# Input projections by token tiles: units of 512 weight columns and half the contraction instead of 256 columns and all of it

## The reference

```
even:  p = h @ w_in          # 1024 x 3072
       q, k, v, g, u, sv = split(p, 6)      # 512 columns each
odd:   p = h @ w_in          # 1024 x 2608
       q  = rope(p[..., :1024]);  kv = p[..., 1024:2560]  (cmp, sel, win: k 256, v 256 each; k gets rope)
       gates = sigmoid(p[..., 2560:])       # 48
```

## Time and profile before

| | us |
|---|---|
| three runs, median | 1634.25 |
| lowest, highest | 1633.77, 1636.83 |
| span of the profiled execution | 1633.6 |
| TensorE busy | 1589.3 (97%) |
| VectorE busy | 797.2 (49%) |
| ScalarE busy | 679.8 (42%) |
| GpSimd busy | 229.6 (14%) |

### The profile page before, as it was taken

How to read it: one execution, slowest core, us unless ns; L and a number is a source line. 1 busy time by engine, 2 the same in 40 slices (tenths; PEclk the granted TensorE clock), 3 DMA queues, 4 the chain that set the end, 5 groups by cost and what they waited for, 6 DMA issues and landing times.

```text
span 1633.6 us, 31861 instructions
## 1 busy us (share of the span) xinstructions
PE 1589.3 (97%) x13307; PEld 1453.7 (89%) x13307; DVE 797.2 (49%) x1314; ACT 679.8 (42%) x1302; POOL 229.6 (14%) x574
## 2 busy tenths in 40 slices
PE   8999999999999999999999899999999999999998
PEld 7999988699999999998999666667989999999997
DVE  5755452556531555337334576743165552355523
ACT  3222134455532554324332566654355552354522
POOL 3000010300000000002013345432020000000001
PEclk9999999999999999999999999999999999999999
DMA  7222328122233232332334400034202323323231
GB/s 223 83 75 78 104 73 206 25 78 77 84 93 99 78 84 80 94 95 54 112 106 92 167 16 2 1 94 99 80 27 78 87 69 103 95 82 99 58 89 55
DMA packets 187417, 138.50 MB, mean 85 GB/s; under 512 B 11376, under 2 KB 178576, under 8 KB 187248
## 3 DMA queue, kind: packets, MB, share of 16 engines
q1 hardware_dynamic: 179424, 113.26, 24.4%
q0 software_dynamic: 7888, 23.79, 5.2%
HBM read 128.21 MB, written 13.01 MB: 86 GB/s over the span
## 4 chain that ended last, share of the span: by engine, by line
PE 89%; DVE 5%; ACT 2%; POOL 1%; issue 1%; DMA 1%; POOLq 0%; SPq 0%; DVEq 0%; ACTq 0%
PE gemm L990 42%; PE gemm L648 18%; PE gemm L659 9%; PE misc L623 6%; PE gemm L1132 2%; PE misc L1163 2%; PE misc L721 1%; PE gemm L707 1%; DVE y L1727 1%; PE misc L1283 1%; PE gemm L745 1%; PE misc L745 1%; PE gemm L677 1%; DVE wL L1693 1%; DMA xin<-in_x_prompt 1%
## 5 line engine op out<-in xcount | busy, mean ns | idle before, releaser
L1693 DVE TENSOR_TENSOR wL<-raw,wH 128x2048 fp32r<-128x2048 f32 (+2 forms) x107 | 222.1, 2076 | 222.8 <-ACT wH L1318 222.7
L990 PE MATMUL gemm<-hH,wH 128*128 128x272 f32 x1280 | 268.5, 291 | 0.1
L990 PE MATMUL gemm<-hH,wL 128*128 128x272 f32 x1280 | 264.8, 288 | 0.0
L990 PE MATMUL gemm<-hL,wH 128*128 128x272 f32 x1280 | 264.0, 288 | 0.0
L990 PEld LDWEIGHTS gemm<-hH,wH 128*128 128x128 f32 x1280 | 200.5, 188 | 6.2 <-issue 4.9
L1318 ACT ACTIVATE wH<-raw 128x2048 fp32r<-128x2048 f32 (+2 forms) x107 | 185.2, 1731 | 48.3 <-PE gemm L648 31.1
L990 PEld LDWEIGHTS gemm<-hL,wH 128*128 128x128 f32 x1280 | 201.0, 188 | 0.0
L990 PEld LDWEIGHTS gemm<-hH,wL 128*128 128x128 f32 x1280 | 200.0, 189 | 0.0
L1959 DVE SCALAR_TENSOR_TENSOR conv<-up,rows_t,conv 128x560 f32<-128x560 f32 x88 | 70.6, 802 | 209.2 <-ACT conv L1318 209.2
L1318 ACT ACTIVATE up<-gemm 128x32 f32<-128x32 f32 (+2 forms) x264 | 66.0, 324 | 176.0 <-PE gemm L990 153.7
L648 PE MATMUL gemm<-hH,wH 128*128 128x272 f32 (+1 forms) x624 | 133.0, 294 | 0.8 <-issue 0.5
(11 more groups left out here) (370 smaller groups left out, 2849.1 us busy)
## 6 DMA issues: line engine op xcount, KB each, us to landing
raw<-in_f_w_in SPq DMA_DIRECT2D x88, 512.0 KB, 5.0
raw<-in_f_w_out SPq DMA_DIRECT2D x32, 704.0 KB, 4.6
raw<-in_e_w_in SPq DMA_DIRECT2D x12, 1024.0 KB, 5.2
raw<-in_o_w_in SPq DMA_DIRECT2D x10, 1024.0 KB, 5.2
raw<-in_e_w_out SPq DMA_DIRECT2D x4, 1024.0 KB, 6.4
raw<-in_o_w_out SPq DMA_DIRECT2D x16, 256.0 KB, 6.4
pages<-in_cache_cmp POOLq DMA_DIRECT2D x10, 256.0 KB, 4.8
xin<-in_x_prompt SPq DMA_DIRECT2D x2, 1024.0 KB, 7.7
```

Source lines behind the costliest of these rows:

```text
L990: ins = pe.matmul(gemm[odd][:, n, 0:TH], w, x[:, k, n * TH:(n + 1) * TH], start=(k == 0 and part == 0), stop=(k == nk - 1 and part == 2))
L1693: order(dve.tensor_tensor(unit_view(wL, u), unit_view(raw, u), unit_view(wH, u).bitcast(F32), ALU.subtract), lo_ready)
```

## The change

The token units become pairs. A pair has 512 weight columns, and its two units ("parts") hold one half of the contraction each (k-blocks 0 to 3, then 4 to 7). A part moves 512 columns per matmul, 4 k-blocks x 3 x 4 tiles. The four prompt tiles take the four gemm banks, one each (`token_bank`), and stay there from part 0 to part 1; only part 1 has chunks (4), so its tiles are copied out one by one. The number of units stays as it is: 4 in the even layer, 10 in the odd one.

The sample tokens are four f32 matmuls of 512 columns per part, in bank b4, at the start of a part; in the very first part of each layer they come after the tiles. They replace tile 0 in the first units too. SyncE's load of unit u+2 waits for the sample matmuls of unit u in all parts now. A part 0 waits for VectorE's sum of the pair before (`sample_ev`). ScalarE's wait for part 0 is a semaphore of its own (`part_done`).

On VectorE the sample rows are 512 wide and come once per pair; the ropes of a q pair (two groups of 4 heads) both follow the pair's last tile. In the even layer `sample_rows` of the `v` pair moves out of the layer norm to ahead of its scaling. In the odd layer ScalarE takes the four turned blocks in one go after the high half of unit 5, and TensorE waits for the first of them ahead of unit 4 (`cp_ev`). The transposes of `vcPt` move to bank b6.

```diff
-    for n in (10, 11, 4, 5, 0, 1, 2, 3, 8, 9, 6, 7):
-        units.append(("even_in", 0, n, 5 if n in (4, 5, 10, 11) else 2))
+    def by_tokens(kind, columns):
+        return [(kind, 0, (columns, part), 4 * part) for part in range(2)]
+
+    units = by_tokens("even_tok", 2560) + by_tokens("even_tok", 1024)
+    for n in (0, 1, 2, 3, 8, 9, 6, 7):
+        units.append(("even_in", 0, n, 2))
...
+    for columns in (1024, 1536, 2048):
+        units += by_tokens("odd_tok", columns)
+    units.append(("odd_in", 0, 10, 1))
+    for columns in (0, 512):
+        units += by_tokens("odd_tok", columns)
...
+        def token_bank(u, t):
+
+            return gemm[(FIRST_CHUNK[u] + t - 1) % 2][:, (t - 1) // 2, :]
...
-                    if UNITS[u - 2][3] == NT and u - 2 not in (E_IN, O_IN):
-                        sp.wait_ge(gemm_done, FIRST_CHUNK[u - 2] + 2)
+                    if u - 2 in TOKEN_UNITS:
+                        sp.wait_ge(sample_read, READS_AFTER + parts_before(u - 2) + 1)
...
+            def take_bank(c, shared):
+
+                count = c // 2 - (1 if shared else 0)
+                if count > 0:
+                    pe.wait_ge(evacuated[c % 2], count)
...
+            def token_products(u, k, t):
+
+                ts, at = tile_start(t), (k % 4) * 512
+                wh, wl = wH[:, u % 2, at:at + 512], wL[:, u % 2, at:at + 512]
                 xh, xl = hH[:, k, ts:ts + P], hL[:, k, ts:ts + P]
                 for part, (x, w) in enumerate(((xh, wh), (xh, wl), (xl, wh))):
+                    ins = pe.matmul(token_bank(u, t), x, w, start=(k == 0 and part == 0), stop=(k == DC - 1 and part == 2))
...
+            def sample_products(u, xs):
+
+                part = token_part(u)
+                if part == 0 and u != E_IN:
+                    pe.wait_ge(sample_ev, SAMPLES_AFTER + parts_before(u) // 2)
+                if u in (E_IN, O_IN):
+                    pe.wait_ge(xs_ready, XS_AFTER + (1 if u == E_IN else 2))
+                for q in range(4):
+                    ins = pe.matmul(b4[32 * q:32 * q + 32, :], xs[:, 4 * part + q, :], raw[:, u % 2, q * 512:(q + 1) * 512],
+                                    start=(part == 0), stop=(part == 1))
+                order(ins, sample_read)
+
+            def token_unit(u, xs, fill=None):
+
+                part, c0 = token_part(u), FIRST_CHUNK[u]
+                ks = range(4 * part, 4 * part + 4)
+                after_tokens = u - 1 in TOKEN_UNITS
+                if part:
+                    sample_products(u, xs)
+                elif fill is None:
+                    sample_products(u, xs)
+                if part == 0:
+                    for t in range(1, 3):
+                        take_bank(c0 + t - 1, after_tokens)
+                if fill is not None:
+                    for t in range(3, 5):
+                        take_bank(c0 + t - 1, True)
+                    for k in ks:
+                        pe.wait_ge(h_ready, DC * fill + k + 1)
+                        for t in range(1, NT):
+                            ins = token_products(u, k, t)
+                    order(ins, part_done)
+                    sample_products(u, xs)
+                    return
+                for t in range(1, NT):
+                    if part == 0 and t >= 3:
+                        take_bank(c0 + t - 1, True)
+                    for k in ks:
+                        ins = token_products(u, k, t)
+                    if part:
+                        order(ins, gemm_done)
+                if part == 0:
+                    order(ins, part_done)
...
+                    if n == 4:
+                        pe.wait_ge(cp_ev, 1)
+                    token_unit(u, xsO, 3 if n == 0 else None)
...
+                if u - 2 in TOKEN_UNITS and token_part(u - 2) == 0:
+                    act.wait_ge(part_done, PARTS_AFTER + parts_before(u - 2) // 2 + 1)
+                elif u >= 2:
                     act.wait_ge(gemm_done, FIRST_CHUNK[u - 1])
...
-                    if n == 4:
-                        take_rows_turned(t - 1)
+                if n == 4:
+                    for t in range(4):
+                        take_rows_turned(t)
...
-                sample_rows(E_IN + 2, vN[0:NS, 0, 0:256])
...
-                    if t == NT - 1:
-                        sample_rows(E_IN + 3, vN[0:NS, 0, 256:512])
...
+                elif n == 1:
+                    sample_rows(u, svn[0:NS, 0, :])
+                elif n == 3:
+                    sample_rows(u, vN[0:NS, 0, :])
...
+                for g in ((0, 1) if columns < D else (0,)):
                     dve.wait_ge(trig_in, 32)
```

More of the change, by code:

```diff
@@ L159, with token_part, parts_before @@
 O_IN = F0 + FFN_UNITS
-O_OUT = O_IN + 11
+O_OUT, O_GATES = O_IN + 11, O_IN + 6
 F1 = O_OUT + 4
+TOKEN_UNITS = [u for u in range(len(UNITS)) if UNITS[u][0] in ("even_tok", "odd_tok")]
+def token_part(u):
+    return UNITS[u][2][1]
+def parts_before(u):
+    return TOKEN_UNITS.index(u)
 class Order:
@@ L496, in unit_source @@
                                w[j, g2, :, :, 256 * n:256 * n + 256])
+            elif kind in ("even_tok", "odd_tok"):
+                columns, part = n
+                w = {"even_tok": a["e_w_in"], "odd_tok": a["o_w_in"]}[kind][0]
+                yield (raw[:, s, :].rearrange("p (k n) -> p k n", k=DC // 2),
+                       w[512 * part:512 * part + 512, columns:columns + 512].rearrange("(k p) n -> p k n", p=P))
             elif kind in ("even_in", "even_out"):
@@ L660, in token_products @@
                 return ins
[L662 to L690, removed]
-                        if k == DC - 1:
-                            order(ins, gemm_done)
+            def sample_products(u, xs):
[8 more added lines that the diff above has]
+                order(ins, sample_read)
@@ L1375, in _ @@
                 split_hi(u + 1)
-                what = UNITS[u][2]
+                if n in (0, 1, 2):
+                    continue
+                what = UNITS[u][2] if n > 3 else None
                 for j in range(UNITS[u][3]):
                     c = FIRST_CHUNK[u] + j
-                    if what < 4:
+                    if n > 3 and what < 4:
                         rc = 2 * what + j
@@ L1547, in _ @@
                     split_hi(u + 1)
-                what = UNITS[u][2]
-                if what == 10:
+                if u == O_GATES:
                     c = FIRST_CHUNK[u]
@@ L1862, in sample_rows @@
             def sample_rows(u, dst, view=lambda ps: ps):
-                c = FIRST_CHUNK[u] + 1
-                ps = [view(gemm[c % 2][32 * q:32 * q + 32, 0, 0:256]) for q in range(4)]
-                dve.wait_ge(gemm_done, c + 1)
+                ps = [view(b4[32 * q:32 * q + 32, :]) for q in range(4)]
+                dve.wait_ge(sample_read, READS_AFTER + parts_before(u) + 1)
                 order(dve.tensor_copy(dst, ps[0]))
@@ L1995, in _ @@
                 if n == 0:
-                    order(dve.memset(kvN[:, 0, 256:3 * 512], 0.0))
+                    order(dve.memset(kvN[:, 0, :], 0.0))
                 elif n == 1:
@@ L1999, in _ @@
                     order.wait()
-                what = UNITS[u][2]
-                if n and what < 4:
-                    sample_rows(u, heads_of(0, what)[0:NS], lambda ps: ps.rearrange("p (r d) -> p r d", r=R))
-                elif n and what < 10:
-                    sample_rows(u, kvN[0:NS, 0, (what - 4) * 256:(what - 3) * 256])
-                if what in (4, 6, 8, 0, 1, 2, 3):
-                    if n:
-                        order.wait()
-                    for last in (FIRST_CHUNK[u + 1] - 2, FIRST_CHUNK[u + 1] - 1):
-                        dve.wait_ge(evacuated[last % 2], last // 2 + 1)
+                if u not in TOKEN_UNITS or token_part(u) == 0:
+                    continue
+                columns = UNITS[u][2][0]
+                if columns < D:
+                    sample_rows(u, queries_of(0, columns // 512)[0:NS], lambda ps: ps.rearrange("p (g r d) -> p g r d", g=2, r=R))
+                else:
+                    sample_rows(u, kvN[0:NS, 0, columns - D:columns - D + 512])
+                order.wait()
+                for last in (FIRST_CHUNK[u + 1] - 2, FIRST_CHUNK[u + 1] - 1):
+                    dve.wait_ge(evacuated[last % 2], last // 2 + 1)
+                for g in ((0, 1) if columns < D else (0,)):
                     dve.wait_ge(trig_in, 32)
-                    if what < 4:
-                        x = qN[:, :, (what // 2) * 512:(what // 2) * 512 + 512].rearrange("p t (r g d) -> p t r g d", r=R, g=2)[:, :, :, what % 2, :]
+                    if columns < D:
+                        x = qN[:, :, columns:columns + 512].rearrange("p t (r g d) -> p t r g d", r=R, g=2)[:, :, :, g, :]
                     else:
-                        x = kvN[:, :, (what - 4) * 256:(what - 3) * 256].rearrange("p t (g d) -> p t g d", g=G)
+                        x = kvN[:, :, columns - D:columns - D + 256].rearrange("p t (g d) -> p t g d", g=G)
```

96 lines of the change are left out of this document (35 added, 61 removed).

## The result

| | median | lowest to highest | runs |
|---|---|---|---|
| before | 1634.02 us | 1632.39 to 1640.01 | 20 |
| after | 1637.45 us | 1634.73 to 1641.48 | 20 |

The ratio is 1.0019, 95% interval 1.0011 to 1.0027: slower by 3.4 us at the medians, where 2.9 faster was forecast. The profiled run took 1641.31 us with a span of 1639.5. It lies 3.9 us above its own median, and 2.8 of that is the start: its first projection matmul comes at 32.43 us, not at 29.63, behind a half-clock stretch at 12.4 us, where the change altered nothing.

The account below looks back on a forecast made before the run. TensorE's work and the waits that stop it bound the two input projections. Gains 2.7 + 3.6 = 6.3 us, less 3.4 for the clock, net 2.9: span 1633.6 becomes 1630.7, median 1631.3; range 1625 to 1636.5.

Parts of the forecast that it names:

- Second stage: Odd layer's input projection, from 749.57 us: walked unit by unit through its waits to 890.9, a gain of 3.6 us.
- rival E: Whole kernel: waits longer than taken, such as a load 3 us later in the first stage, cancel the gain; 1634.3, chance 0.12.
- The load: Second stage, unit 2's weights: 5.2 us to land after the sample block; TensorE then loses 1.7 us at its next sample block.
- The step: Both projections: 512-column matmuls start 0.225 us apart, from 213.3 ns plus 12 fixed; a part takes 10.81 us against 11.42.
- Rival C: Both projections: matmul cost goes with the columns, 0.238 us at 512, a part 0.6 us more; 1637.4, chance 0.06.
- The clock: Whole kernel: four waits of 1.7 to 2.5 us bring two stretches at half speed, costing 3.4 us; bounds 0 and 13.6.
- Small terms: Second stage: each new sample block taken at 1.1 us, and an idle of 2.5 us after the fourth unit's transposes.
- VectorE as the pace of the first stage: First stage: VectorE's layer norm chain, not TensorE, stops it from 57.0 us on; stage gain 2.7 us.
- the gate mask: First stage's end: TensorE waits 2.3 us, to 87.5, for VectorE's mask of the gate weights; before it waited 0.78.
- The wait for the compressed keys' bank: Second stage, n = 4: TensorE idles 2.5 us after the transposes until ScalarE has emptied b4 of the turned rows.
- the end of the stage: Second stage: about 4.3 us from the last projection matmul to the query transposes, one rope more; before 2.46.
- the third wait: Second stage: TensorE idle 1.7 us before the third sample block, released by VectorE's sample add.

Follow-up runs that it names:

- sweep: Changed kernel plus streams of 32 matmuls at ten widths and some variants, added to read their steps; 1737.47 us, which only says matmuls were added.
- phi_late: Changed kernel with GpSimd's four loads of phiK2 and phiV2 issued behind the first store of rows; 1629.76 us, 0.9974 of before.
- phi_rows: phi_late with ScalarE taking the first turned sample row ahead of its split of the next unit; 1628.67 us, 0.9970 of before.
- sample_early: Changed kernel with the first unit's sample matmuls ahead of the last k block in either projection, phi loads unmoved; 1630.43 us, 0.9974 of before.
- phi_split256: phi_late with each 512-column matmul of the 14 token-major units issued as two of 256 columns; 1634.01 us, 0.9997 of before.
- before_phi_late: Kernel before with only the four phi loads issued after the first store; 1639.57 us, 1.0035 of before.
- three_fixes: Changed kernel with late phi loads, early sample matmuls and the first turned sample row taken early; 1626.14 us, 0.9945 of before.
- early_rows: Changed kernel with early sample matmuls and the first turned row taken early, phi loads unmoved; 1626.45 us, 0.9957 of before.
- three_moved: three_fixes with VectorE's split of output weights behind the turned queries' copies and the qS memset ahead of the last ropes; 1625.85 us, 0.9957 of before.
- four_fixes: three_fixes with the last two ropes done for tiles 0 to 3 first, then for tile 4; 1627.40 us, 0.9960 of before.
- five_fixes: three_fixes with both the parted last ropes and the moved split and memset on VectorE; 1622.57 us, 0.9935 of before.
- even_only: Kernel before with the new form in the first (even) projection only, the second as before; 1629.33 us, 0.9969 of before.

## Why the prediction was wrong

The failed step is in "Second stage": "The load of unit 2, held by the sample block until 761.5, gives its low half at 771.3". The issue time was right (761.22), the landing was not: 9.00 us and not 5.2. The 5.2 is a median over loads that mostly run alone, and the prediction never asked what GpSimd's queue was doing at 761, though the profile before has the phi loads there (759.72 to 763.06). That the sample block would hold the load it saw; that this put the load off from 726.05, where nothing else moves, into the midst of the phi loads, it did not. It even named the danger in rival E, "a load that lands 3 us later", but put it in the first stage. Against the forecast of the second stage (141.3 us at full clock; 152.17 measured):

- **The load**: wait of 5.26 for 1.7, +3.6.
- **The step**: 0.2348 us in the kernel (full-speed units of 48 take 11.21 to 11.33, mean 11.27) for 0.225, so 0.46 a part, ten parts: +4.6. The line through 256 and 272 columns (7 ns apart in the sweep, 6 in the earlier trace rows) was carried too far. A unit saved 0.33 us, not 0.6, and that from another start than the prediction's 11.42: the 0.119 of the earlier trace rows is a step within 51 matmuls, and over a whole unit before took 11.60, so 11.60 became 11.27. Rival C had the direction; measured 0.2348 lies three quarters of the way to its 0.238.
- **The clock**: two units of 12.87 and 12.88 for 11.27 and a sample block of 1.87 for 1.0: +4.1 in this stage, where the forecast booked 3.4 for the whole kernel. Three stretches, two of them from the longer wait on.
- **Small terms**: both first sample blocks in 1.85 for 2.4, eight more at 1.00 for 1.1, fifth unit 2.26 for 2.5: -1.6.

These make 10.7 of 10.9. Two slips of the prediction's sums are small: twelve blocks of 1.07 and fourteen of 1.1 differ by 2.6 us and not 2.2, a figure that the time does not use, and the terms named for the low half of unit 2, 761.5 + 5.2 + 1.9 + 2.3, make 770.9 and not 771.3. The rival's number, 1637.4, was met by the measured 1637.45, but not by its mechanism alone: phi_late has the same step and is 4.5 us faster than before, so the dear step ate gain without making the change slower. The load and the clock did that, some 8 us.

What was right: VectorE as the pace of the first stage. TensorE ran longer there than forecast and waited less for the gate mask, 0.83 for 2.3, and the stage ended 56.98 us after its start (forecast 57.87). The 0.9 is VectorE's chain, summed a little too long. The wait for the compressed keys' bank (2.26 for 2.5) and the end of the stage (900.99 - 896.65 = 4.34 for 4.3) were right to the tenth, and phi_late shows the third wait right too once the phi loads are out of the way (1.41 for 1.7).

The clock stays open in part. Each wait is short, and the same one does not always bring half clock. By the granted clock of the profiles:

| wait | us | half clock begins by 2 us behind its end in |
|---|---|---|
| before the third unit | 6.05 | sweep (3 stretches; its load took 9.8 us) |
| before the third unit | 5.26 | after (2 stretches, from 777.1) |
| before the third unit | 1.41, 1.45 | not in phi_late, phi_rows |
| before the fifth unit | 2.26 | after, sample_early; not phi_late, phi_split256, sweep |
| fourth unit, before_phi_late | 2.59 | 2 stretches |
| ahead of the query transposes | 2.39 | phi_late, sample_early, three_fixes, early_rows, three_moved; not after, phi_rows, phi_split256 |
| the same | 0.93, 0.94 | not in four_fixes, five_fixes |
| within them, behind the split | 2.00 to 2.04 | after, phi_rows, four_fixes; not before, even_only, before_phi_late, phi_split256 |

The three longest waits had it, 2.0 to 2.4 us is near a coin toss, and there is one profile of each kernel. The half-clock stretch at 12 to 14 us is in five of the thirteen profiles beside the sweep's, at a place where no kernel differs: chance too, and worth 2 to 3 us in the run that has it.

## What to carry to other kernels

A load's landing time is read for the moment of issue and not from the median of its kind. When an edit adds a reader to a buffer, the next load into it is issued later: look up when it went out before, when it will go out now, and what the other queues have under way at that time. When two transfers meet, put the one that somebody waits for first in line; here 2.5 us of issue time decided 3.6 us of landing and a wait of 5.26. And after removing a wait, look down the same engine's queue for work that is not urgent; a short wait in a profile at half clock can be a longer one at full clock.

## What the hardware showed that I had not expected

- A fp32r matmul with a new 128-wide stationary tile each time took 111 ns up to 224 columns, 118 at 256 and 0.445 ns more for each column from there on. Plain f32 took 429 ns a row at 512 columns, with two rows for each matmul. The Trainium skill, "TensorE: Matmul & The Clock Gate", section "Back-to-back issue gap", gives 216 ns at 512 columns by its formula; the sweep measured 232 and the kernel 235, so here the measurement stands against it.
- 1 MB of weights landed in 5.14 us with one more weight load 0.9 us behind it, and in 9.00 with that and 1 MB of phi loads begun 2.4 us ahead, though in 5.4 when it went out 0.2 us before the first of them.
- A rope instruction of VectorE took 0.32 us at 160 columns, 0.28 at 128 and 0.18 at 32: about 1.1 ns a column and 0.15 fixed, so parting a rope in two is cheap beside the wait it hides.
